# Order of the set-up work of token group 0 in a hybrid decoder layer on eight cores

## What is computed

```python
mod = silu(c) @ w_ada + b_ada                # 6 x 1024 per sequence: shifts, scales, gates
h = rmsnorm(x, g) * (1 + sc1) + sh1          # 2048 x 1024
proj = h @ w_in                              # q_lat 384 | kv_lat 256 | k_rope 32 | swa q 512, k 128, v 128
q = rmsnorm(q_lat, g_qa) @ w_qb              # 8 heads of 64 + 32 (rotary)
kv = rmsnorm(kv_lat, g_kva) @ w_kvb          # 8 heads: 64 key, 64 value; rotary key shared
y_mla = causal_softmax(q, k) @ v             # dense, in blocks of 128 queries
y_swa = softmax([scores in a band of 128, sink]) @ v   # 8 heads, 2 key/value heads, sink per head
x = x + g1 * (concat(y_mla, y_swa) @ w_o)
x = x + g2 * (relu(h2 @ w_up)**2 @ w_down)   # h2: normed and modulated as h
return rmsnorm(x, final_g)
```

## Time and profile before

| | |
|---|---|
| median of 3 runs | 965.85 us (965.66 to 966.04) |
| the profiled execution | 968.15 us, its span 966.5 us (core 7) |
| spans of the eight cores | 960.3 to 966.5 us |
| PE busy | 871.5 us (90% of the span) |
| DVE, ACT, POOL busy | 346.4, 515.9, 117.9 us |
| share of PE in the chain that ended last | 78% (ACT 7%, DVE 5%, DMA 4%) |

### The profile page before, as it was taken

One profiled execution on the slowest core, in us unless ns is written; L12 is line 12 of the kernel. 1 busy time (PEld: TensorE's weight loads), 2 busy tenths in 40 slices (PEclk: granted clock), 3 DMA queues, 4 the chain that ended last, 5 costly groups with the idle time before them and its releaser, 6 DMA issues.

```text
span 966.5 us, 12968 instructions; the slowest of 8 cores (960.3 to 966.5 us)
## 1 busy us (share of the span) xinstructions
PE 871.5 (90%) x4449; PEld 389.6 (40%) x4449; DVE 346.4 (36%) x560; ACT 515.9 (53%) x765; POOL 117.9 (12%) x130
## 2 busy tenths in 40 slices
PE   2766688987898889999999999999999999999994
PEld 1323233432353334444444444444444444444441
DVE  0253646434535452223672222111222221112456
ACT  3062485667568868877688333444333334445543
POOL 6000111111111111122100000000000000003431
PEclk9767789987999999999999999999999999999998
DMA  9992222362212042202939004040041300000224
GB/s 194 169 182 67 61 61 44 55 131 44 44 34 44 1 88 87 88 1 88 203 59 170 5 1 77 11 87 1 1 87 24 63 1 1 1 1 1 87 87 175
DMA packets 13743, 63.49 MB, mean 66 GB/s; under 512 B 1776, under 2 KB 2032, under 8 KB 9968
## 3 DMA queue, kind: packets, MB, share of 16 engines
q0 software_dynamic: 8352, 36.41, 22.3%
q1 hardware_dynamic: 5328, 26.27, 8.0%
HBM read 90.69 MB, written 8.39 MB: 103 GB/s over the span
## 4 chain that ended last, share of the span: by engine, by line
PE 78%; ACT 7%; DVE 5%; DMA 4%; issue 4%; POOL 1%; DVEq 0%; ACTq 0%; POOLq 0%
PE ps L492 67%; PE ps L965 5%; PE ps L918 5%; DMA arena<-wada 4%; ACT arena L949 3%; DVE arena L545 1%; DVE arena L1268 1%; ACT arena L981 1%; PE ps L925 1%; ACT arena L666 1%; ACT arena L496 1%; ACT arena L663 0%; ACT arena L1218 0%; DVE arena L847 0%; DVE arena L1001 0%
## 5 line engine op out<-in xcount | busy, mean ns | idle before, releaser
L492 PE MATMUL ps<-arena 128*128 128x512 bf16 (+5 forms) x3713 | 778.3, 353 | 79.2 <-DMA arena<-wada 21.9
L492 PEld LDWEIGHTS ps<-arena 128*128 128x128 bf16 (+2 forms) x3713 | 326.4, 99 | 485.7 <-issue 163.8
L1250 DVE SCALAR_TENSOR_TENSOR arena<-ps,arena 128x512 f32<-128x512 f32 x128 | 95.8, 749 | 313.5 <-PE ps L492 313.5
L949 ACT ACTIVATE arena<-ps 128x1024 bf16<-128x1024 f32 x158 | 158.5, 1021 | 81.8 <-PE ps L492 51.1
L1237 ACT ACTIVATE arena<-ps 128x512 f32<-128x512 f32 x128 | 76.2, 595 | 211.5 <-PE ps L492 211.0
L918 PE MATMUL ps<-arena 128*128 128x512 bf16 (+1 forms) x320 | 87.2, 355 | 5.0 <-ACT arena L949 3.9
L965 PE MATMUL ps<-arena 128*128 128x512 bf16 (+1 forms) x320 | 87.2, 355 | 0.0
L1238 ACT ACTIVATE arena<-arena 128x512 bf16<-128x512 f32 x128 | 80.5, 629 | 11.9 <-ACT arena L1237 0.2
L957 POOL TENSOR_TENSOR arena<-arena 128x512 bf16<-128x512 f32 x32 | 42.3, 1322 | 264.4 <-ACT arena L956 180.9
L1098 ACT ACTIVATE arena<-arena 128x512 bf16<-128x512 f32 x56 | 35.3, 630 | 44.5 <-DVE arena L1250 34.9
L977 DVE COPY arena<-ps 64x512 f32<-64x512 f32 x32 | 22.0, 687 | 75.6 <-PE ps L965 55.6
...
## 6 DMA issues: line engine op xcount, KB each, us to landing
arena<-wada POOLq DMA_DIRECT2D x24, 512.0 KB, 7.5
arena<-xt SPq DMA_DIRECT2D x8, 1024.0 KB, 9.4
...
arena<-wup POOLq DMA_DIRECT2D x8, 1024.0 KB, 12.4
arena<-wdn POOLq DMA_DIRECT2D x8, 1024.0 KB, 18.4
out<-arena SPq DMA_DIRECT2D x12, 512.0 KB, 2.7
...
```

The costliest lines, as they stand in the source:

```text
L492: S.op("pe", lambda h: h.matmul(bk(bank, rows, cols), lhsT=lhsT, rhs=rhs, start=start, stop=stop), r=r, w=[bankb[bank]])
L949: S.op("act", lambda h: h.activation(out=PT[p][:, :, c0:c1], in_=PS[:, b0:b0 + 2, c0:c1], func=AF.Exp, scale=sc), r=[bankb[b0], bankb[b0 + ...
L1250: S.op("dve", lambda h, b=b, fb=fb: h.scalar_tensor_tensor(out=X1T[G][:, fb, :], in0=bk(b), scalar=MODCOL[:, 40 + fb:41 + fb], in1=X1T[G][ ...
```

## The change

The eight `ESK` parts and their exponential are recorded right after the first activation of the start. To allow this, `ESK` gets the phase "s" as well; the placement then exchanges memory between `ESK`, the key tile of group 0 and the first up-weights, and everything else keeps its place. In the preparation of group 0, the copies of the three query latents go from ACT to DVE, their squares are recorded behind the key/value norm, `qstat` moves ahead of the bias of the banded keys, and the 16 `SHB` tiles follow that bias, ahead of the rotary additions. In the filler of group 0 the query heads 4 to 7 and all value groups stand ahead of the sum of x's squares, and the modulation blocks 8 to 11 leave the next group's preparation and are dealt between the scalings of x.

```diff
--- before.py
+++ after.py
@@ -391,7 +391,7 @@
         bSWQ = [Buf(f"SWQ_{c}", a_SWQ) for c in range(4)]
         SMASK, bSM = tile1("SMASK", [128, 2, 2, 512], BF16, "sa012x3y")
         TRI, bTRI = tile1("TRI", [128, 256], BF16, "sa012x3y")
-        ESK, bESK = tile1("ESK", [128, 512], F32, "a012x3y")
+        ESK, bESK = tile1("ESK", [128, 512], F32, "sa012x3y")
         PT, bPT = [], []
         for i in range(3):
             v, b = tile1(f"PT{i}", [128, 2, 512], BF16, "012x3y")
@@ -532,6 +532,8 @@
                     in_=xt_d[G * 128:(G + 1) * 128, i * 2048:(i + 1) * 2048]), bXD[i], r=list(after),
                       w=[bXD[i]] + bXT[4 * i:4 * i + 4])
 
+        bankr = [Buf(f"bankr{i}") for i in range(8)]
+
         def x_square(k):
             S.op("act", lambda h: h.activation(out=SQX[k], in_=XT[:, k, :], func=AF.Square),
                  r=[bXD[k // 4], bXT[k]], w=[bSQX[k]])
@@ -648,6 +650,8 @@
         def csx_load(G):
             S.dma("sp", lambda h: h.dma_start(out=CSX, in_=csx_d[:, G * 512:(G + 1) * 512]), bCSX, w=[bCSX])
 
+        squares_later = []
+
         def a_streams(G, rot):
             lat = {}
 
@@ -659,12 +663,21 @@
                     if m < 2:
                         S.op("act", lambda h: h.activation(out=LATF[:, m, :], in_=bk(b), func=AF.Identity, bias=BCOL[:, m:m + 1]),
                              r=[bankb[b], bBCOL], w=[bLF[m]])
+                    elif G == 0:
+                        S.op("dve", lambda h: h.tensor_scalar(out=QRAW[:, m - 2, :], in0=bk(b), scalar1=GQKV[:, m - 2:m - 1],
+                                                              scalar2=BCOL[:, 10 + m:11 + m], op0=ALU.mult, op1=ALU.add),
+                             r=[bankb[b], bCOLS, bBCOL], w=[bQR[m - 2], bankr[b]])
                     else:
                         S.op("act", lambda h: h.activation(out=QRAW[:, m - 2, :], in_=bk(b), func=AF.Identity,
                                                            scale=GQKV[:, m - 2:m - 1], bias=BCOL[:, 10 + m:11 + m]),
                              r=[bankb[b], bCOLS, bBCOL], w=[bQR[m - 2]])
-                    S.op("act", lambda h: h.activation(out=SQ[s], in_=bk(b), func=AF.Square, bias=BCOL[:, m:m + 1]),
-                         r=[bankb[b], bBCOL], w=[bSQ[s]])
+                    def square():
+                        S.op("act", lambda h: h.activation(out=SQ[s], in_=bk(b), func=AF.Square, bias=BCOL[:, m:m + 1]),
+                             r=[bankb[b], bBCOL] + ([bankr[b]] if G == 0 and m >= 2 else []), w=[bSQ[s]])
+                    if G == 0 and m >= 2:
+                        squares_later.append(square)
+                    else:
+                        square()
                 return f
 
             def stat_items(ms, i, nf, then):
@@ -758,6 +771,13 @@
         S.op("dve", lambda h: h.memset(EPSC, EPS), w=[bEPS])
         S.op("dve", lambda h: h.memset(ONESB, 1.0), w=[bONES])
         S.op("act", lambda h: h.activation(out=SILU, in_=CCOL, func=AF.Silu), r=[bCOLS], w=[bSILU])
+        S.op("act", lambda h: h.activation(out=SK8, in_=SINK, func=AF.Exp), r=[bCOLS], w=[bSK8])
+        for hh in range(8):
+            kv, g = hh // 4, hh % 4
+            S.op("dve", lambda h, hh=hh, kv=kv, g=g: h.tensor_scalar(
+                out=ESK[kv * 64:kv * 64 + 64, g * 128:(g + 1) * 128], in0=ONESB[kv * 64:kv * 64 + 64, :],
+                scalar1=SK8[kv * 64:kv * 64 + 64, hh:hh + 1], scalar2=None, op0=ALU.mult),
+                 r=[bSK8, bONES], w=[bESK])
         x_dma(0)
         csx_load(0)
         first = [4, 5, 6, 7, 0, 1, 2, 3]
@@ -833,21 +853,24 @@
         for f in held[:5]:
             f()
         run_items(kvstat)
+        for f in squares_later:
+            f()
         held[5]()
+        run_items(qstat)
         bias_cols([5], 0)
+        for k in range(8):
+            for i, col in enumerate((MODCOL, SHL)):
+                S.op("dve", lambda h, k=k, i=i, col=col: h.tensor_scalar(
+                    out=SHB[:, i, k, :], in0=ONESB, scalar1=col[:, k:k + 1], scalar2=None, op0=ALU.mult),
+                     r=bMOD[0:4] + [bSHL, bONES], w=[bSHB])
+
         swk_, swq_, swv_ = swa_streams(0, rot0)
-        for part in [qstat] + rope[:2] + [swk_]:
+        for part in rope[:2] + [swk_]:
             run_items(part)
         for part in kp + vp + rope[2:]:
             run_items(part)
         run_items(qp[0])
         run_items(qp[1])
-        for k in range(8):
-            for i, col in enumerate((MODCOL, SHL)):
-                S.op("dve", lambda h, k=k, i=i, col=col: h.tensor_scalar(
-                    out=SHB[:, i, k, :], in0=ONESB, scalar1=col[:, k:k + 1], scalar2=None, op0=ALU.mult),
-                     r=bMOD[0:4] + [bSHL, bONES], w=[bSHB])
-
         def bias_v(bank):
             for k in range(8):
                 for i in range(2):
@@ -857,14 +880,6 @@
 
         ada_dma(8, 0)
         ada_dma(9, 1)
-        S.op("act", lambda h: h.activation(out=SK8, in_=SINK, func=AF.Exp), r=[bCOLS], w=[bSK8])
-        for hh in range(8):
-            kv, g = hh // 4, hh % 4
-            S.op("dve", lambda h, hh=hh, kv=kv, g=g: h.tensor_scalar(
-                out=ESK[kv * 64:kv * 64 + 64, g * 128:(g + 1) * 128], in0=ONESB[kv * 64:kv * 64 + 64, :],
-                scalar1=SK8[kv * 64:kv * 64 + 64, hh:hh + 1], scalar2=None, op0=ALU.mult),
-                 r=[bSK8, bONES], w=[bESK])
-
 
         MLA_SCALE = float(96 ** -0.5)
         SWA_SCALE = 0.125
@@ -1133,8 +1148,8 @@
                 bq = [(5.0, lambda: bias_cols([6, 7, 8, 9], rotB.next()), None)]
                 bv = [(5.0, lambda: bias_v(rotB.next()), None)]
                 groups = [qp[2], qp[3], bq, swq_[0], swq_[1]]
-                groups += spread([swq_[2], swq_[3], bv, swv_[0], qp[4]], [[x] for x in square_items])
-                groups += [x_sum_stream(rotB), flat(swv_[1:])] + spread(qp[5:], scales) + [swap, xnext]
+                groups += spread([swq_[2], swq_[3], bv, swv_[0]] + qp[4:] + swv_[1:], [[x] for x in square_items])
+                groups += [x_sum_stream(rotB)] + spread(adas(8, 12), scales) + [swap, xnext]
             else:
                 k_, q_, v_ = swa_streams(G, rotB)
                 groups = [swap] + [k_] + q_ + v_
@@ -1149,7 +1164,7 @@
                     body = spread(body[3:], [[x] for x in square_items])
                     later = lats[:3] + body + kp + vp + qp[:5] + [x_sum_stream(rotB)] + qp[5:]
                     if G == 0:
-                        filler += flat(groups + spread(later, adas(8, 12)))
+                        filler += flat(groups + later)
                     else:
                         filler += flat(spread(groups + later, adas(12, 20)))
             else:
```

## The result

The changed kernel takes 971.64 us (median of 6 runs, 970.47 to 972.99) against 965.94 for the kernel before, run beside it (6 runs, 964.88 to 968.52): a ratio of 1.0053, 95% interval 1.0040 to 1.0066. It is slower by about 5 us; 964.6 was forecast, with a range up to 967.8.

What follows compares the result with a forecast made beforehand. The slowest core bounds the kernel, with two PE pauses in group 0 on its path; -0.4 + 1.4 - 1.4 + 0.7 + 0.9 = 1.2 us gained, from a median of 965.85 to 964.6 us, range 961.2 to 967.8.

Steps and rivals of the forecast that it cites:

- First pause: PE's idle at 72 to 79.7 us: first scores 3.9 us later, bias columns 1.8 us earlier, clock back at 81.2.
- the first rival: Clock stays up through the pause near 72 us: lead grows by 2.6 us, result 962.0 us; chance 0.30.
- the lead at the third exponential: Time gained after PE's pause near 72 us, from earlier bias columns and clock return: 87.2 - 83.4 = 3.8 us.
- Logarithm and issue: Before PE's second pause: logarithm of x at 101.8 us, block 10's fetch issued on POOL at 107.2.
- the landing: Block 10's fetch beside an x load takes 7.2 us, so the block is there at 114.4 us.
- -0.4: PE's second pause is not removed: it ends at 114.4 us where it ended at 114.0.
- Block 10 lands late: Rival: x's 1 MB shares the engines with blocks 10 and 11; slower, 967.8 to 970 us; chance 0.14.
- +1.4: Four modulation blocks leave the later stretch, 2.7 us in all, half counted as real: 1.4 us gained.
- -1.4: Blocks 10 and 11 are still to be done when PE's second pause ends: 1.4 us lost.
- +0.7: Blocks 10 and 11, as tiny matmuls, lose nothing to the low clock after the second pause: 0.7 us gained.
- +0.9: The clock's fall at 132 to 138 us has an even chance to go: half of 1.9 us gained.
- Everything from group 1 on keeps its order: From token group 1 on, the order of the work stays as before; no time was counted for it.

Runs made afterwards that it cites:

- The run with the fetch first: The changed kernel with GpSimd's (POOL's) division of the first banded pair queued behind the fetches of blocks 10 and 11, not ahead; 968.00 us (1.0000).
- without the x load: The changed kernel with the load of x for group 2 held back until block 11 has been used; 969.45 us (1.0033).
- kernels of 954.59: The changed kernel with blocks 8 and 9 between the scalings, none among group 1's latents, 10 and 11 a group later; 954.59 us (0.9869).
- 946.97 us: The changed kernel with blocks 8, 9 between scalings, 10, 11 a group later, and the 16 broadcast tiles behind the query tiles' bias columns; 946.97 us (0.9786).

## Why the prediction was wrong

**First pause: right in its place, off in the clock's return.** The broadcast tiles delay the first scores: 3.9 us were forecast, 22.4 - 18.5 = 3.9 were measured on core 7. The bias columns follow without a wait. The clock fell, as forecast, on all eight cores, so the first rival, by which it stays up, came true on none. But the prediction had it return 7.5 us after PE's restart, as before. It took 8.7 to 9.4 us on cores 0, 1, 5 and 7, where the third exponential comes 9.2 to 9.6 us after the first, and 2.6 to 4.7 us on the others, where it comes 7.2 to 7.7 after. On core 7 the lead at the third exponential is 3.0 us (33.2 us after the first latent copy in place of 36.2), where 3.8 was forecast.

**Logarithm and issue: nearly right.** The logarithm of x was forecast 50.4 us after the first latent copy (101.8 - 51.4) and came 49.2 to 51.6 after it, on core 7 51.4. The fetch of block 10 was forecast 55.8 us after it and came 55.2 to 57.6, on core 7 57.4. The division on POOL took 2.33 us, where I had taken 1.5.

**The step that failed: the landing, behind an issue that was late as well.** I took 7.2 us, from a block fetched beside an x load; on core 7 it was 9.4 to the landing and 9.7 to the first matmul (109.44 to 119.11). With the issue 1.6 us late, the pause ended 4.1 us later than forecast (67.1 in place of 63.0 us after the first latent copy; 62.6 before). "-0.4" should have been -4.5. The mechanism was the forecast's, and the sign in it was that of the rival *Block 10 lands late*; that rival asked for a landing of 10.4 us or more, and did not see that the queue in front of the fetch and the landing could miss together. The run with the fetch first shows that this is the loss: asked for 4.5 us sooner, the block lands sooner, and the stretch to group 1 falls from 88.4 to 81.4 us. The rule of the Trainium skill that I had weighed ("DMA: Bandwidth & Descriptors", section "Anatomy of one DMA — SWDGE (gpsimd) path": 2.0 us plus the bytes at 436 GB/s, by which I had estimated 3.2 us) is not borne out: without the x load the fetch still took 4.9 to 8.2 us to land, so the row was the better guide and still too kind.

**The terms behind the pause: +1.4, -1.4, +0.7 and +0.9 are 1.6 in sum, and nothing came.** On core 7 group 1's first exponential comes 55.2 us after the end of the pause (119.11 to 174.34), 55.3 before (114.01 to 169.32). Which term was wrong can't be read off part by part. From the end of the pause to the first latent copy it took 10.8 us (119.11 to 129.92) in place of 6.7 (114.01 to 120.69), and from there to group 1 44.4 in place of 48.6; but the first of these parts holds three exponentials in place of one, the second 11 in place of 13, so attention work has moved from one to the other. The fall of the clock that had an even chance to go did not go: on core 7 the clock is 0.50 from 142 to 144 and from 156 to 158 us. The new pause near 150 us, which the prediction had not seen, stands also in the kernels of 954.59 and 946.97 us.

**"Everything from group 1 on keeps its order": not quite, and worth little.** The filler's pieces are handed out by a budget per unit whose remainder is carried on; with another list ahead, some pieces of the later groups stand one place off. The last stretch is 687.2 us in place of 686.3, and over the kernels it has two levels, 685.4 to 686.3 and 687.2 to 688.0. Behind its first exponential ACT has one order in all kernels of the lower level and another in all of the upper: a copy that stands 0.6 us ahead of that exponential before stands 1.7 us behind it after. So a part of the 0.9 us is where I cut. Counted from the 61st exponential it is 0.2 us (709.4 and 709.2), from the 101st -0.4 (639.6 and 640.0).

On core 7 the end of the pause and the missing terms give 4.1 + 1.6 - 0.1 = 5.6 us, and that is what it misses at group 1: 4.4 us later than before, counted from the first latent copy, where 1.2 sooner was forecast. The time misses by 7.0 us (971.64 - 964.6). The other 1.4 us are not located; core 7 itself takes 1.1 us less behind group 1's first exponential (796.1 in place of 797.2). The sum had no term for the better question, which the experiments answered: how many blocks may stand between the scalings without a fetch to wait for, and whether the tiles have a third place.
